# Mixture of experts inside a float32 network: tokens in groups of 32, expert weights unsplit and read once

## The chip, the cores and the metric

One core of one Trainium2 chip runs the whole program. The metric is device time in microseconds (us) of one execution, median of several; lower is better. Engines: PE is TensorE, DVE is VectorE, ACT is ScalarE, POOL is GpSimd, SP is SyncE, which only starts transfers here.

## The reference, cut to what matters

Two blocks run one after the other in float32 on 256 latent tokens of 1024 features (and 256 context tokens in part of the first block). The change is in one place only, the mixture of experts that ends the first block:

```python
def _moe_swiglu(h, router_w, router_b, w1, w3, w2):
    logits = (h @ router_w) + router_b
    top_vals, top_idx = lax.top_k(logits, 2)
    top_w = jax.nn.softmax(top_vals, axis=-1)
    gates = jnp.sum(one_hot(top_idx, 8) * top_w[..., None], axis=-2)
    out = jnp.zeros_like(h)
    for e in range(8):
        out = out + gates[..., e:e + 1] * ((silu(h @ w1[e]) * (h @ w3[e])) @ w2[e])
    return out
```

h is 256 x 1024; w1[e] and w3[e] are 1024 x 2816, w2[e] is 2816 x 1024. Each token uses two of eight experts, so there are 512 pairs of token and expert, spread over the experts as the data has it. The eight experts hold 276.8 MB of weights.

## The kernel before

All of the network before and after the experts is a stream of weight tiles of 128 x 1024 float32 (`w_raw`). For every tile ACT writes a rounded copy in the type fp32r (`w_hi`, line 265), DVE writes the remainder (`w_lo`, line 269), and PE multiplies three times (`pe_triple`, lines 306 to 308: hi by hi, lo by hi, hi by lo); the sum of the three fp32r products stands in for one product in float32.

**Routing.** `dve_router` finds each token's two experts and its slot. Slots lie in blocks of 128: eight blocks, one for each expert, and three overflow blocks that an expert with more than 128 pairs takes (NBLK = 11, 1408 slots). `onehot` holds the token-by-slot matrices. `pe_gather` multiplies tokens by `onehot` and so gathers every slot's token vector, once for the hi and once for the lo part (line 2192); ACT writes `x_hi` (line 2204), DVE `x_lo` (line 2214).

**Experts.** For each of the 11 blocks the weights of its expert are read from HBM again, in 66 tiles of 512 KB (`sp_experts`, line 2054, ring `mraw` of six tiles; the overflow blocks take their expert's number from the register `e0`). ACT and DVE split each tile into `mhi` and `mlo` (lines 2324 and 2328). On PE a block of 128 slots is stationary and the weights move, 512 columns at a time. A block has 11 steps of 256 hidden columns (`step`): `hidden` makes 8 x 3 matmuls, `turn` transposes the 256 gated columns of the step before in two transposes (line 2243), `out` makes 4 x 3 matmuls into the output. ACT and DVE make silu and product (lines 2337 and 2402) and the hi and lo parts of the turned values (lines 2341 and 2407). Loops: blocks outside, steps inside, and the order on every engine is written by hand in `step`; five steps of each block are written out, the rest is a hardware loop.

**Back to tokens.** The block's output, scaled by its gates (`gsl`, from `slot_gates`, line 2282), overwrites the block's part of `x_hi` and `x_lo`; `spread` multiplies it by the transposed one-hot matrix (`s_main`, `s_last`) and adds it up in PSUM (line 2262). `dve_experts_out` adds the sum into `hT`, and the norm behind it starts with ACT's `normx` and PE's line 530. The constants of the second block (`conb`) are loaded together with the slot numbers as the experts begin (`pool_conb`).

A place far from the experts matters as well: `pe_quad` (line 662), which makes the rows of the modulation at the start of the program. It puts 32 stationary columns each into four column groups of the array, one after another, and each group has plain float32 weights of its own moving through it.

Of the kernel before, what the change touches and what calls it, by code (L numbers as in the profile page):

```python
# [17 lines left out]
F32 = mybir.dt.float32  # L18
F32R = mybir.dt.float32r
# [23 lines left out]
NBLK = 11  # L43
SLOTS = NBLK * P
FSTEP = 256
NSTEP = DFF // FSTEP
XT = 6 * NSTEP
MOE_RAW = 6
MOE_RING = 4
# [29 lines left out]
for _n, _w in CONSTS_B:  # L79
# [6 lines left out]
          ("na_out", 8), ("moe", XT * NBLK)]  # L86
# [7 lines left out]
for _n, _w in STREAM:  # L94
# [3 lines left out]
MOE = XT * NBLK  # L98


SECOND = {"tok_ps": ("mod_ps", 1), "moe_rank": ("tot_ps", 1), "gat_hi": ("mb_ss", 1), "gat_lo": ("tm_ps", 1),
          "sp_ps": ("xtm_ps", 1), "x_acc": ("btm_ps", 1), "tok_hi": ("cv", 1), "x_hi": ("dt_l", 1),
          "y_hi": ("aneg", 1), "sp_sb": ("dt_u", 1), "moe_a": ("dt_rows", 1), "moe_mask": ("dt_abs", 1),
          "tok_lo": ("dt_w", 1), "x_lo": ("mb_sq", 2), "onehot": ("mb_ms", 1), "y_out": ("mb_done", 1),
          "slotno": ("lora", 32)}


def build(nc, io):
    with ExitStack() as es:
# [108 lines left out]
        def sp_stream(sp):  # L218
# [18 lines left out]
            repeat(sp, BASE["moe"], RING, more, first=first)  # L237
            sp_experts(sp)
            first = BASE["moe"] + MOE
            sp.wait_ge(tile_used.sem, first + RING)  # L240

            def later(n, j):
                slot = (first + j) % RING
                if not (isinstance(n, int) and n < first + RING):
                    sp.wait_ge(lo_ready.sem, n - (RING - 1))
                sp.dma_start(raw[:, slot, :], w[one(n - MOE)].rearrange("o p c -> p (o c)")
                             ).then_inc(raw_loaded[slot].sem, 16)
# [11 lines left out]
        rounds_apart = [0]  # L259

        def act_split(act, n, i3, slot):

            act.wait_ge(raw_loaded[slot].sem, i3 * 16 + (16 - rounds_apart[0] * 16))
# [1743 lines left out]
        def cb(name):  # L2007
            return conb[:, BCOL[name][0]:BCOL[name][1]]

        conb_at = END - 64 - (NCONB * 4 + 63) // 64 * 64  # L2010
        mhi = sb("mhi", [P, MOE_RING, 1024], F32R, at=ring0)
        mlo = sb("mlo", [P, MOE_RING, 1024], F32R, at=ring0 + 4096 * MOE_RING)
        slotno = sb("slotno", [P, SLOTS], at=ring0)
        tok_hi = sb("tok_hi", [P, 2, D], F32R, at=ring0 + 4096 * MOE_RING)
        tok_lo = sb("tok_lo", [P, 2, D], F32R, at=ring0 + 4096 * MOE_RING + 8192)
        s_at = ring0 + 8192 * MOE_RING
        s_last = sb("s_last", [P, 3, SEG], F32R, at=s_at)
        (lgt, t1, oh1, oh2, slt, msk, wv, ovf, oin, oex, dlt, eov, pq, xj, xi, gov, t24, gsl, _r) = lay(s_at + 3072, [
            ("lgt", [P, 2, NE]), ("t1", [P, 2, NE]), ("oh1", [P, 2, NE]), ("oh2", [P, 2, NE]), ("slt", [P, 2, NE]),
            ("msk", [P, 2, NE]), ("wv", [P, 8]), ("ovf", [P, NE]), ("oin", [P, NE]), ("oex", [P, NE]),  # L2020
            ("dlt", [P, NE]), ("eov", [P, NE]), ("pq", [P, 4]), ("xj", [P, 3]), ("xi_f", [P, 3]), ("gov", [P, 2, 3]),
            ("t24", [P, 3, NE]), ("gsl", [P, NBLK])])
        assert _r <= ring0 + 3 * 4096 * RING, _r
        x_at = area
        x_hi = sb("x_hi", [P, KT, SLOTS], F32R, at=x_at)
        x_lo = sb("x_lo", [P, KT, SLOTS], F32R, at=x_at + 4 * KT * SLOTS)
        mraw = sb("mraw", [P, MOE_RAW, 1024], at=x_at + 8 * KT * SLOTS)
        one_at = x_at + 8 * KT * SLOTS + 4096 * MOE_RAW
        onehot = sb("onehot", [P, 2, SLOTS], F32R, at=one_at)
        s_main = sb("s_main", [P, NE, SEG], F32R, at=one_at + 8 * SLOTS)  # L2030
        assert one_at + 8 * SLOTS + NE * SEG * 4 <= conb_at
        normx = sb("normx", [P, KT, SEG], at=x_at + 8 * KT * SLOTS)
        xi = sb("xi", [P, 3], mybir.dt.int32, at=s_at + 3072 + 6 * 64 + 6 * 32 + 2 * 32)
        xg_hi = sb("xg_hi", [P, 2, 2, P], F32R, at=g_at)
        xg_lo = sb("xg_lo", [P, 2, 2, P], F32R, at=g_at + 2048)
        xraw = deep_loaded
        GROUPS_X = ((0, 512), (512, 1024), (1024, SLOTS))
        PEEL = 5

        def spread_of(b):  # L2040
            return s_main[:, b, :] if b < NE else s_last[:, b - NE, :]

        def slots_of(b):
            return slice(b * P, (b + 1) * P)

        def sp_experts(sp):
            w = io["wexp"]

            def load(m, slot, idx):
                if not (isinstance(m, int) and m < MOE_RAW):
                    sp.wait_ge(lo_ready.sem, m + (BASE["moe"] - MOE_RAW + 1))
                sp.dma_start(mraw[:, slot, :], w[one(idx)].rearrange("o p c -> p (o c)")
                             ).then_inc(xraw[slot].sem, 16)
            sp.wait_ge(*S("arena_free2").next("sp"))
            before = None
            for b in range(NBLK):
                if b < NE:
                    e0 = b * XT  # L2060
                else:
                    if b == NE:
                        sp.wait_ge(*S("overflow").next("sp"))
                    e0 = sp.value_load(xi[0:1, b - NE:b - NE + 1], min_val=0, max_val=NE - 1) * XT
# [1153 lines left out]
```

## Time and profile before

| | |
|---|---|
| median of 3 runs | 3622.81 us (3614.82 to 3623.66) |
| profiled execution, span | 3619.5 us, 3.3 below the median |
| mean granted clock of TensorE | 0.967 |
| PE busy | 3402.0 us, 94% |
| DVE, ACT busy | 2497.9 us, 1878.7 us |
| HBM read | 719.57 MB, 199 GB/s over the span |
| expert weights read (`mraw`) | 726 transfers of 512 KB |

The profile has one execution. Its page gives no time of that execution beside the span, so sums are made against the span, and the 3.3 us between it and the median is carried along. PE's busy time overstates its use, because the ends of pipelined matmuls are modelled: the distance from one start to the next is the figure to read, and the timeline of PE has it. In a row of the timeline, two numbers lead: the start in the span and the time covered. One plain float32 matmul stands there as two records, one fp32r matmul or transpose as one.

### The profile page before, as it was taken

How to read it: one execution, taken by the hardware profiler on the slowest of the kernel's cores; microseconds unless marked ns; L12 is line 12 of the kernel's file. 1: busy time of each engine (PE TensorE's matmuls, PEld its weight loads, DVE VectorE, ACT ScalarE, POOL GpSimd, SP SyncE). 2: the span in 40 equal slices, each digit the busy share in tenths (PEclk: the TensorE clock that was granted, in tenths of full speed). 3: DMA queues.
4: the chain of work that ended last, by engine and by line, in shares of the span. 5: the costliest groups of instructions: out<-in, count | busy, mean ns of one | idle time of the engine just before them, and what ended most of it. 6: DMA issues, size and time to landing. Idle time of an engine off the chain costs nothing.

```text
span 3619.5 us, 70952 instructions
## 1 busy us (share of the span) xinstructions
PE 3402.0 (94%) x27148; PEld 3001.8 (83%) x27148; DVE 2497.9 (69%) x3327; ACT 1878.7 (52%) x2493; POOL 7.6 (0%) x17
## 2 busy tenths in 40 slices
PE   5987988899999988999999999999999999999998
PEld 3865857789898867888888888887998899998898
DVE  3778575555555367899999999997558555557555
ACT  3323231234444354788888888886445644444633
POOL 0000000000000000000000000000000000000000
PEclk8997989999999998999999999999999999999999
DMA  5225041035456303999999999996553354553354
GB/s 202 90 102 192 4 171 37 20 128 184 152 181 210 107 31 127 328 363 361 359 363 362 361 361 363 359 362 224 187 184 117 122 183 154 188 183 123 109 182 156
DMA packets 199351, 723.31 MB, mean 200 GB/s; under 512 B 21888, under 2 KB 25472, under 8 KB 198784
## 3 DMA queue, kind: packets, MB, share of 16 engines
q1 hardware_dynamic: 198576, 714.01, 55.4%
q0 software_dynamic: 592, 6.69, 0.5%
q8 instruction: 135, 2.21, 0.2%
q14 instruction: 48, 0.39, 0.0%
HBM read 719.57 MB, written 1.05 MB: 199 GB/s over the span
## 4 chain that ended last, share of the span: by engine, by line
PE 84%; DVE 9%; ACT 3%; DMA 2%; issue 1%; SPq 1%; DVEq 0%; ACTq 0%
PE ps L306 24%; PE ps L307 24%; PE ps L308 24%; DMA ada_late<-wada 1%; PE ps L1571 1%; PE ps L662 1%; PE ps L530 1%; PE ps L1568 1%; PE ps L1562 1%; PE ps L2243 1%; DVE w_lo L269 1%; PE ps L2192 1%; DVE tt L1659 1%; PE ps L2262 1%; ACT w_hi L265 1%
## 5 line engine op out<-in xcount | busy, mean ns | idle before, releaser
L269 DVE TENSOR_TENSOR w_lo<-w_raw,w_hi 128x1024 fp32r<-128x1024 f32 x529 | 647.4, 1225 | 717.8 <-ACT w_hi L265 714.4
L265 ACT ACTIVATE w_hi<-w_raw 128x1024 fp32r<-128x1024 f32 x529 | 558.6, 1059 | 794.2 <-PE ps L308 738.4
L306 PE MATMUL ps<-a_hi,w_hi 128*128 128x256 f32 (+1 forms) x3012 | 901.4, 299 | 54.1 <-DVE a_lo L557 24.6
L2328 DVE TENSOR_TENSOR mlo<-mraw,mhi 128x1024 fp32r<-128x1024 f32 x726 | 876.8, 1224 | 90.4 <-ACT mhi L2324 61.2
L308 PE MATMUL ps<-a_hi,w_lo 128*128 128x256 f32 (+1 forms) x3012 | 899.9, 299 | 0.0
L307 PE MATMUL ps<-a_lo,w_hi 128*128 128x256 f32 (+1 forms) x3012 | 899.8, 299 | 0.0
L2324 ACT ACTIVATE mhi<-mraw 128x1024 fp32r<-128x1024 f32 x726 | 770.6, 1062 | 178.9 <-PE ps L308 151.4
L306 PEld LDWEIGHTS ps<-a_hi,w_hi 128*128 128x128 f32 x3012 | 583.2, 194 | 78.0 <-issue 52.0
L307 PEld LDWEIGHTS ps<-a_lo,w_hi 128*128 128x128 f32 x3012 | 577.7, 192 | 16.5 <-issue 0.5
L308 PEld LDWEIGHTS ps<-a_hi,w_lo 128*128 128x128 f32 x3012 | 577.4, 192 | 14.7
L306 PE MATMUL ps<-mhi,x_hi 128*128 128x512 f32 x968 | 395.0, 408 | 1.9 <-DVE mlo L2328 1.9
L308 PE MATMUL ps<-mhi,x_lo 128*128 128x512 f32 x968 | 383.8, 397 | 0.0
L307 PE MATMUL ps<-mlo,x_hi 128*128 128x512 f32 x968 | 383.1, 396 | 0.0
L306 PE MATMUL ps<-g_hi,w_hi 128*128 128x256 f32 x1056 | 298.9, 283 | 4.5 <-DVE g_lo L465 4.5
L307 PE MATMUL ps<-g_lo,w_hi 128*128 128x256 f32 x1056 | 298.7, 283 | 0.0
L308 PE MATMUL ps<-g_hi,w_lo 128*128 128x256 f32 x1056 | 298.5, 283 | 0.0
L308 PEld LDWEIGHTS ps<-mhi,x_lo 128*128 128x128 f32 x968 | 182.6, 189 | 44.8
L306 PEld LDWEIGHTS ps<-mhi,x_hi 128*128 128x128 f32 x968 | 182.3, 188 | 39.3 <-issue 2.2
L307 PEld LDWEIGHTS ps<-mlo,x_hi 128*128 128x128 f32 x968 | 182.9, 189 | 37.8
L306 PEld LDWEIGHTS ps<-g_hi,w_hi 128*128 128x128 f32 x1056 | 202.2, 192 | 5.5 <-issue 5.5
L308 PEld LDWEIGHTS ps<-g_hi,w_lo 128*128 128x128 f32 x1056 | 202.3, 192 | 0.0
L307 PEld LDWEIGHTS ps<-g_lo,w_hi 128*128 128x128 f32 x1056 | 202.1, 191 | 0.0
(503 smaller groups left out, 4360.4 us busy)
## 6 DMA issues: line engine op xcount, KB each, us to landing
mraw<-wexp SPq DMA_DIRECT2D x726, 512.0 KB, 5.3
w_raw<-wstream SPq DMA_DIRECT2D x529, 512.0 KB, 3.3
ada_late<-wada SPq DMA_DIRECT2D x80, 512.0 KB, 6.1
ada_raw<-wada SPq DMA_DIRECT2D x16, 512.0 KB, 9.0
bia<-bias POOLq DMA_DIRECT2D x1, 4096.0 KB, 13.2
con<-consts SPq DMA_DIRECT2D x1, 1824.0 KB, 16.0
conb<-constsb POOLq DMA_DIRECT2D x1, 1224.0 KB, 8.0
hT<-ctxT SPq DMA_DIRECT2D x1, 1024.0 KB, 12.5
```

The costliest lines, as they stand in the source:

```text
L265: nc.scalar.activation(whi[:, slot, :], raw[:, slot, :], ACT.Copy).then_inc(hi_ready.sem, 1)
L269: nc.vector.tensor_tensor(wlo[:, slot, :], raw[:, slot, :], whi[:, slot, :].bitcast(F32), ALU.subtract).then_inc(lo_ready.sem, 1)
L306: nc.tensor.matmul(out, lhs[0], rhs[0], start=start, stop=False, skip_group_check=skip)
L307: nc.tensor.matmul(out, lhs[0], rhs[1], start=False, stop=False, skip_group_check=skip)
L308: return nc.tensor.matmul(out, lhs[1], rhs[0], start=False, stop=stop, skip_group_check=skip)
L530: last = nc.tensor.matmul(ps[:, 4, 0:SEG], ones[:], (work or normw)[:, k, :], start=(k == 0), stop=(k == KT - 1))
L662: last = nc.tensor.matmul(ps[32 * j:32 * j + 32, bank + half, :], cvp[:, k0 + j, :], tile[:, half * 512:(half + 1) * 512], start=(k0 == 0) ...
L1562: heads_of(d, lambda d, m, e: nc.tensor.matmul(ps[hp(e), d, col(m)], nl[hp(e), lv % 2, d, m, :], tt[hp(e), d, 0, m, :], start=True, stop=True)
L1568: heads_of(d, lambda d, m, e: nc.tensor.matmul(ps[hp(e), 2 + d, col(m)], tt[hp(e), d, 1, m, :], xs[hp(e), d, m, :], start=True, stop=True))
L1571: heads_of(d, lambda d, m, e: nc.tensor.matmul(ps[hp(e), 2 + d, col(m, 1)], xs[hp(e), d, m, :], tt[hp(e), d, 1, m, :], start=True, stop=Tr ...
L2324: nc.scalar.activation(mhi[:, slot, :], mraw[:, rslot, :], ACT.Copy).then_inc(hi_ready.sem, 1)
L2328: nc.vector.tensor_tensor(mlo[:, slot, :], mraw[:, rslot, :], mhi[:, slot, :].bitcast(F32), ALU.subtract).then_inc(lo_ready.sem, 1)
```

## The change

**Slots** lie in groups of 32 instead of blocks of 128: eight base groups, one for each expert, and NX = 15 extra groups, which go to whatever expert has more than 32, 64, ... pairs; 23 groups, 736 slots. Four groups side by side make a "quad" of 128 slots, so there are NQ = 6 quads, the last with three groups.

**Weights** are neither split nor read again. A "set" holds, for all eight experts at once, one piece of 128 x 512 float32 (2 MB, two transfers of 1 MB); there are 88 sets for the hidden layer (11 steps of 8) and 44 for the output (two halves of 22), 132 in all, in a ring of three. The matmuls are plain float32 with 32 stationary columns: in each set PE goes through the six quads (`quad`), and each group of a quad sits in its own column group, with its own expert's weights moving. The base groups read the set directly. Since the extra groups' experts are known only at run time, ACT and DVE copy their weights out of the set into `wx` first (6 copies of 128 x 512 on ACT, 9 on DVE for each set, in four parts), at an address held in a register. Quad i (i from 2) waits for part i-2; part j of the next set waits for quad j+2 of this one.

**Order.** The hidden layer of all slots comes first (`gT` keeps the turned values of all 736 slots and 2816 columns), then the output layer in two halves of 512 columns. At the end of each eight sets the six banks are emptied by silu and product, and in the first set of the next step `turn` puts two transposes behind each quad. `spread` of the first half runs between the sets of the second. `x`, hidden values and weights have no hi and lo parts any more; only the final `y_hi`, `y_lo` keep them. Nothing in the stage is a hardware loop. `conb` is loaded behind the experts.

```diff
-NBLK = 11
-SLOTS = NBLK * P
+GS = 32
+NX = 15
+SLOTS = (NE + NX) * GS
+NQ = 6
+SETS1 = NSTEP * KT
+SETS = SETS1 + 2 * FT
+SET_RING = 3
+X_ACT = ((0,), (4, 5), (8, 9), (12,))
+X_DVE = ((1, 2, 3), (6, 7), (10, 11), (13, 14))
...
+        def sp_set_free(sp, n):
+            sp.wait_ge(S("set_base").sem, based(n, 1))
+            sp.wait_ge(S("wx_act").sem, copied(X_ACT, n, 3))
+            sp.wait_ge(S("wx_dve").sem, copied(X_DVE, n, 3))
...
+            for n in range(SETS):
+                if n >= SET_RING:
+                    sp_set_free(sp, n - SET_RING)
+                for half in range(2):
+                    sp.dma_start(wsets[n % SET_RING][:, 4 * half:4 * half + 4, :].rearrange("p e c -> p (e c)"),
+                                 io["wexp"][2 * n + half]).then_inc(set_loaded[n % SET_RING].sem, 16)
...
+            def quad(n, i, lhs, first, last):
+                if i >= 2:
+                    pe.wait_ge(S("wx_act").sem, copied(X_ACT, n, i - 2))
+                    pe.wait_ge(S("wx_dve").sem, copied(X_DVE, n, i - 2))
+                for j in range(4 if i < NQ - 1 else 3):
+                    g = 4 * i + j
+                    w = wsets[n % SET_RING][:, g, :] if g < NE else wx[:, g - NE, :]
+                    done = nc.tensor.matmul(ps[32 * j:32 * j + 32, i, :], lhs[:, group(g)], w, start=first, stop=last,
+                                            skip_group_check=True)
+                done.then_inc(*S("set_base" if i < 2 else "set_more").one)
...
+            for s in range(NSTEP):
+                for k in range(KT):
+                    n = s * KT + k
+                    set_in(pe, n)
+                    for i in range(NQ):
+                        if s and k == 0:
+                            pe.wait_ge(*S("h_prod").next("pe"))
+                        quad(n, i, xT[:, k, :], k == 0, k == KT - 1)
+                        if s and k == 0:
+                            turn((s - 1) * NQ + i)
...
+            for h in range(2):
+                for f in range(FT):
+                    n = SETS1 + h * FT + f
+                    set_in(pe, n)
...
+                    for i in range(NQ):
...
+                        quad(n, i, gT[:, f, :], f == 0, f == FT - 1)
...
+                    if h == 1 and f < NQ:
+                        spread(f)
+            pe.wait_ge(*S("x_out").next("pe"))
+            for q in range(NQ):
+                spread(q)
...
+        def copies_of(n, j, evacuate, copy):
+            if n > 0 and j == 0:
+                for i in (0, 1):
+                    evacuate(n - 1, i)
+            if n > 0:
+                evacuate(n - 1, j + 2)
+            if n < SETS:
+                copy(n, j)
...
+            ids = {x: dve.value_load(xi[0:1, x:x + 1], min_val=0, max_val=NE - 1) for part in X_DVE for x in part}
+            def copy(n, j):
+                if j == 0:
+                    set_in(dve, n)
+                if n > 0:
+                    quad_done(dve, n - 1, j + 2)
+                for x in X_DVE[j]:
+                    nc.vector.tensor_copy(wx[:, x, :], wsets[n % SET_RING][:, one(ids[x]), :].rearrange("p o c -> p (o c)")
+                                          ).then_inc(*S("wx_dve").one)
```

`pe_gather` makes one sum of hi and lo in PSUM, for 512 and then 224 slots (32 matmuls each) instead of two sums for 512, 512 and 384 (96 matmuls).

On PE, in the middle of the expert stage of the kernel before, a turn and what follows it (`x_hi`, `x_lo`: slots; `mhi`, `mlo`: weights):

```order
L308 MATMUL ps<-mhi,x_lo 128x512
L2243 MATMUL ps<-ident,g_f 128x128 [waits g_f]
L2243 MATMUL ps<-ident,g_f 128x128
L306 MATMUL ps<-mhi,x_hi 128x512 [waits lo_ready]
L307 MATMUL ps<-mlo,x_hi 128x512
L308 MATMUL ps<-mhi,x_lo 128x512
```

The same place of the changed kernel, the end of the eighth set and the start of the ninth (`wset2`: the set itself, `wx`: copies, `mg`: gated hidden values, `y_pe`: the semaphore for the evacuated turn):

```order
L2239 MATMUL ps<-wx_167,xT_164 32x512 [waits wx_dve,wx_act]
L2239 MATMUL ps<-wx_167,xT_164 32x512 x2
L2239 MATMUL ps<-wset2_159,xT_164 32x512 [waits h_prod,deep_loaded2,mb_rt]
L2239 MATMUL ps<-wset2_159,xT_164 32x512 x3
L2250 MATMUL ps<-ident_61,mg_171 128x128 x2
L2239 MATMUL ps<-wset2_159,xT_164 32x512 [waits h_prod]
L2239 MATMUL ps<-wset2_159,xT_164 32x512 x3
L2250 MATMUL ps<-ident_61,mg_171 128x128 x2
L2239 MATMUL ps<-wx_167,xT_164 32x512 [waits wx_dve,wx_act,h_prod]
L2239 MATMUL ps<-wx_167,xT_164 32x512 x3
L2250 MATMUL ps<-ident_61,mg_171 128x128 [waits y_pe]
```

The three fp32r matmuls of 128 stationary columns are now four plain ones of 32, and a turn stands behind each quad of every eighth set.

On DVE, one set in the changed kernel (before, this engine's place held one `mlo` subtraction of 128x1024 for each tile, waiting for `hi_ready`):

```order
L2421 COPY wx<-wset_157 128x512 [waits set_more,deep_loaded0]
L2421 COPY wx<-wset_157 128x512 x2
L2421 COPY wx<-wset_157 128x512 [waits set_more]
L2421 COPY wx<-wset_157 128x512
L2421 COPY wx<-wset_157 128x512 [waits set_more]
L2421 COPY wx<-wset_157 128x512
L2421 COPY wx<-wset_157 128x512 [waits set_more]
L2421 COPY wx<-wset_157 128x512
```

Nine copies in four parts; each part waits for a quad of the set before (`set_more`), the first for the load as well (`deep_loaded0`).

## Rows read from the trace of the kernel before

**Rows 1.** The page: busy us of each engine, share of the span, instructions.

```profile
PE 3402.0 (94%) x27148; PEld 3001.8 (83%) x27148; DVE 2497.9 (69%) x3327; ACT 1878.7 (52%) x2493; POOL 7.6 (0%) x17
```

**Rows 2.** Windows: us, busy (count) of PE, PEld, DVE, ACT, POOL; PEclk, DMA share, GB/s.

```profile
1500.00:1700.00 200.00, 200.00 (x898) 162.24 (x897) 183.79 (x189) 160.66 (x189) 0.00 (x0) 1.00 0.98 362
```

**Rows 3.** Chain of waits inside the expert stage, shares by line.

```profile
by line: PE ps L306 31.5%; PE ps L308 31.4%; PE ps L307 31.2%; PE ps L2243 2.5%; PE ps L2262 1.4%; DVE mlo L2328 0.7%; DMA mraw<-wexp 0.7%; PE ps L2282 0.5%; PE ps L2272 0.1%; ACT mhi L2324 0.1%; DVE t L2173 0.1%; DVE gov L2174 0.1%; issue 
```

**Rows 4.** Timeline of PE around one turn: start us, us, engine, line, op, count [idle].

```profile
1701.93 0.40 PE L308 MATMUL ps<-mhi,x_lo 128*128 128x512 f32 x1
1702.17 0.38 PE L2243 MATMUL ps<-ident,g_f 128*128 128x128 f32 x2
1702.31 0.48 PE L306 MATMUL ps<-mhi,x_hi 128*128 128x512 f32 x1
1702.62 0.40 PE L307 MATMUL ps<-mlo,x_hi 128*128 128x512 f32 x1
```

**Rows 5.** Timeline of PE: gather, and start of the expert stage.

```profile
1408.74 1.19 PE L2192 MATMUL ps<-onehot,tok_hi 128*128 128x512 f32 x2 [5.85 <-DVE onehot L2154]
...
1412.15 0.62 PE L2192 MATMUL ps<-onehot,tok_hi 128*128 128x512 f32 x2
...
1425.21 0.51 PE L2192 MATMUL ps<-onehot,tok_hi 128*128 128x384 f32 x2
...
1432.89 0.47 PE L306 MATMUL ps<-mhi,x_hi 128*128 128x512 f32 x1 [1.87 <-DVE mlo L2328]
```

**Rows 6.** Timeline of PE at the end of the expert stage.

```profile
2496.45 0.39 PE L308 MATMUL ps<-mhi,xg_lo 128*128 128x512 f32 x1
2496.68 0.28 PE L2262 MATMUL ps<-s_main,x_hi 128*128 128x256 f32 x1
...
2503.32 3.62 PE L530 MATMUL ps<-normx,ones 128*128 128x256 f32 x16
```

**Rows 7.** Page, groups of the expert stage: busy us, mean ns | idle before, releaser.

```profile
L2328 DVE TENSOR_TENSOR mlo<-mraw,mhi 128x1024 fp32r<-128x1024 f32 x726 | 876.8, 1224 | 90.4 <-ACT mhi L2324 61.2
...
L2324 ACT ACTIVATE mhi<-mraw 128x1024 fp32r<-128x1024 f32 x726 | 770.6, 1062 | 178.9 <-PE ps L308 151.4
...
L306 PE MATMUL ps<-mhi,x_hi 128*128 128x512 f32 x968 | 395.0, 408 | 1.9 <-DVE mlo L2328 1.9
```

**Rows 8.** Timeline of PE and its weight loads at the early modulation rows (L662).

```profile
11.73 3.64 PE L662 MATMUL ps<-ada_raw,cvp 128*32 128x512 f32 x16 [11.73 <-DMA ada_raw<-wada]
16.81 1.92 PE L662 MATMUL ps<-ada_raw,cvp 128*32 128x512 f32 x16 [1.43 <-DMA ada_raw<-wada]
...
48.13 3.64 PE L662 MATMUL ps<-ada_raw,cvp 128*32 128x512 f32 x32
...
48.59 0.13 PEld L662 LDWEIGHTS ps<-ada_raw,cvp 128*32 128x32 f32 x4 [0.30 <-issue]
...
50.73 0.13 PEld L662 LDWEIGHTS ps<-ada_raw,cvp 128*32 128x32 f32 x4 [0.30 <-issue]
```

**Rows 9.** Timeline of PE where 64-column matmuls give way to 128-column ones.

```profile
252.89 0.38 PE L1192 MATMUL ps<-wm_b,xdt 128*64 128x128 f32 x2
253.11 0.38 PE L1194 MATMUL ps<-cm_b,hin 128*64 128x128 f32 x2
253.42 0.49 PE L1172 MATMUL ps<-bcx 128*128 128x128 f32 x2
```

**Rows 10.** Timeline of PE at the slot gates, and the clock of that stretch.

```profile
1468.25 3.63 PE L2282 MATMUL ps<-lgt,onehot 128*128 128x1 f32 x32
...
1460.00:1480.00 20.00, 20.00 (x106) 16.98 (x105) 12.06 (x13) 11.04 (x15) 0.00 (x0) 0.91 0.80 277
```

**Rows 11.** Lines with 128x512 float32 from SBUF to SBUF on DVE and ACT: ns min/median/max.

```profile
L1129 DVE TENSOR_SCALAR dd<-dd x8: 426/426/428, 239.4 to 284.3; 128x512 f32<-128x512 f32 x8
...
L574 ACT ACTIVATE normw<-hT x16: 613/616/635, 38.3 to 1166.5; 128x512 f32<-128x512 f32 x16
```

**Rows 12.** Windows: 10 us in which only loads ran (columns as in rows 2).

```profile
24.00:34.00 10.00, 0.00 (x0) 0.00 (x0) 0.00 (x0) 0.00 (x0) 0.00 (x0) 0.50 1.03 408
```

More of the change, by code:

```diff
@@ L2008, in cb @@
             return conb[:, BCOL[name][0]:BCOL[name][1]]
[L2010 to L2016, printed above, removed]
@@ L2048, in sp_experts @@
-        def sp_experts(sp):
[L2049 to L2055, printed above, removed]
-            sp.wait_ge(*S("arena_free2").next("sp"))
[L2057 to L2064, printed above, removed]
-                m = b * XT - 2 if b else 0
-                for q in range(4):
-                    load(m + q, (m + q) % MOE_RAW, e0 + q)
-                for q in range(2 if b else 0):
-                    load(m + 4 + q, (m + 4 + q) % MOE_RAW, before + (XT - 2 + q))
-                with sp.Fori(0, NSTEP - 1) as i:
-                    for j in range(6):
-                        load(i * 6 + (b * XT + 4 + j), (4 + j) % MOE_RAW, i * 6 + (e0 + (4 + j)))
-                before = e0
-            for q in range(2):
-                load(MOE - 2 + q, (4 + q) % MOE_RAW, before + (XT - 2 + q))
@@ L2186, in pe_gather @@
                     i = g * KT + k
[L2187 to L2190 removed]
+                    if i >= 8:
+                        pe.wait_ge(*S("x_act" if i % 2 == 0 else "x_dve").next("pe"))
+                    for tok in (tok_hi, tok_lo):
                         for tt_ in range(2):
[L2192 to L2194 removed]
@@ L2195, in pe_gather @@
-            pe.wait_ge(*S("x_hi").next("pe", 4))
-            pe.wait_ge(*S("x_lo").next("pe", 4))
+                            last = nc.tensor.matmul(ps[:, i % 8, 0:c1 - c0], tok[:, tt_, k * P:(k + 1) * P],
+                                                    onehot[:, tt_, c0:c1], start=(tok is tok_hi and tt_ == 0),
+                                                    stop=(tok is tok_lo and tt_ == 1))
+                    last.then_inc(*S("gat_ps").one)
+            pe.wait_ge(*S("x_act").next("pe", 4))
@@ new lines, in spread @@
+            def spread(q):
+                r = rows_of(q)
+                pe.wait_ge(*S("y_out").next("pe"))
+                for m in range(4):
+                    for part in (y_hi, y_lo):
+                        last = nc.tensor.matmul(ps[:, 6 + m // 2, m % 2 * SEG:(m % 2 + 1) * SEG],
+                                                part[r, q, m * P:(m + 1) * P], spr[r, q, :],
+                                                start=(q == 0 and m % 2 == 0 and part is y_hi),
+                                                stop=(q == NQ - 1 and part is y_lo), skip_group_check=True)
+                    if q == NQ - 1 and m % 2 == 1:
+                        last.then_inc(*S("x_acc").one)
```

552 lines of the change are left out of this document (252 added, 300 removed).

## The prediction, made before the changed kernel ran

> **What bounds the kernel now.** I read the page first, for which engine has most work: PE, 94% busy [rows 1]. Since that figure overstates a pipelined engine, I looked at windows inside the expert stage: PE is at 200.00 of 200 us with a granted clock of 1.00, while DVE is at 184, ACT at 161, and loads run at 362 GB/s, DMA share 0.98 [rows 2]. So four resources are near their ends, and the chain of waits has to say which one leads: 98% of its links are PE's own matmuls and turns, 0.7% loads, 0.7% DVE's `mlo` [rows 3]. The timeline gives PE's true pace: an fp32r matmul of 512 columns starts every 0.235 us [rows 4]. The stage has 121 steps x 36 = 4356 of them, 1024 us at that pace. With gather, turns and spreads it lasts from 1408.7 (first gather matmul, [rows 5]) to 2503.3 (end of the last spread, [rows 6]), 1094.6 us. ACT waited for PE (151 us) more than for loads, and PE waited for DVE for 1.9 us in all [rows 7]. The stage is PE's, with the split on ACT and DVE and the loads close behind.
>
> **The change, part by part.** The rest of the program is untouched, so I sum the stage anew from 1408.7, the same first matmul, because the routing chain before it keeps its number of operations.
>
> *The quads.* 132 sets x 6 quads = 792. The trace has this very instruction: `pe_quad` puts 32 stationary columns each into four column groups, plain float32, 512 columns moving. At 48.13 there are 32 records (16 matmuls) in 3.64 us; the groups of four weight loads start every (50.73 - 48.59) / 5 = 0.428 us [rows 8]. A matmul is two records, so four groups side by side take 2 x 0.428 = 0.856 us. Quads: 792 x 0.856 = 678.0 us. The sixth has three groups and takes the same. Per set that is 5.14 us on PE.
>
> *The turns.* 11 steps x 6 = 66. A turn's two transposes cost 0.14 us, and the matmul behind them 0.31 instead of 0.235, together 0.22 [rows 4]. New is the change between 32 and 128 stationary columns, twice a turn. The nearest row is a change from 64 to 128: two records take 0.31 where their equals take 0.22, so 0.09 [rows 9]. 0.22 + 0.18 = 0.40, x 66 = 26.4 us. Bounds: 0.22 (15 us) and, if each change lets the pipeline run empty as at the end of a burst (0.21, below), 0.64 (42 us). I take 0.40, the row of a change of width.
>
> *Gather.* 64 matmuls instead of 96. The first eight take 3.4 us as now, 24 follow at 0.233 us ((1425.21 - 1412.15) / 56), 32 have 224 columns, 0.11 each in proportion, and 1.0 us for the last evacuation [rows 5]: 3.4 + 5.6 + 3.5 + 1.0, so experts start at 1422.2 instead of 1432.9. No split is waited for at that point.
>
> *Smaller work on PE.* Spreads of the first half, 48 x 0.119 us (56 matmuls from 2496.68 to 2503.32, [rows 6]) = 5.7. One-hot transposes, 12 x 0.07 = 0.8. Slot gates, 46 plain matmuls = 92 records, between 0.03 us (a weight load of 32 columns in a group of four, [rows 8]) and 0.113 us (3.63 / 32, [rows 10]), so 3 to 10 us in all; I take 6, since they have one moving column and their own column groups. Ten changes of width, 1.8. The slot gates also cost clock: around them the mean granted clock is 0.91 over 20 us [rows 10], 1.8 us lost; I carry 2. Together 16.3 us.
>
> *Registers.* ACT and DVE read six and nine expert numbers into registers before their first copy. No row of either engine shows that. Lower bound 0, because quads 0 and 1 (1.7 us) need no copy; upper bound 12, nine loads at some 1.3 us, the price of a full 1024-column operation [rows 7]. I take 4.
>
> *Copies, off the path.* A SBUF-to-SBUF operation of 128x512 is 0.43 us on DVE and 0.62 on ACT [rows 11]: 9 x 0.43 = 3.8 and 6 x 0.62 = 3.7 us a set, inside PE's 5.14. Order matters more than load here: part 0 may start when quad 2 of the set before is done, 2.6 us before the new set, and is needed 1.7 us after its start, so each part has 3 us or so to spare. At the end of a step six silus, six products and six turned evacuations come in between. I followed ACT and DVE through it: the last copy of the step's first set is done about 3.5 us after that set's start on PE, and the last quad, held up by turns, needs it at 5.5. Cover holds; if it failed, each failure would be paid 11 times, not 132.
>
> *Loads.* Set n can be loaded once set n-3 is free, 2 us after its start, and has 13 us until it is needed. So only the rate counts. Nothing but loads running, the trace shows 408 GB/s [rows 12]; 2.097 MB then take 5.14 us, exactly the quads of one set. The turns give slack (8 sets take 43.5 us on PE, 386 GB/s), the last 44 sets give almost none. At 408, loads stay just behind PE, and I cost them at nothing.
>
> *Tail.* After the last quad: silence until ACT's and DVE's scaled evacuation of it, at most 0.7 us each by half of [rows 7], hand-offs 0.4, eight spread matmuls 1.0: 2.8. Before, the stretch from the last expert matmul was 6.9 us, counted in the 1094.6.
>
> Sum: 678.0 + 26.4 + 16.3 + 4 = 724.7; 1422.2 + 724.7 + 2.8 = 2149.7 instead of 2503.3. **That saves 353.6 us**: span 3265.9, and with the 3.3 us of the median, **3269 us**. The median's runs spread over 9 us; 0.3% (11 us) is what I count as no change.
>
> **Rivals.**
>
> *Loads lead.* Only 408 GB/s in a quiet stretch speaks for the cover; under PE, ACT and DVE the trace shows 362 at a DMA share of 0.98 [rows 2], though there PE set the pace. If 362 is the most that the loads give, 129 sets from 1431 on (when set 0 is free) take 270.5 MB / 362 = 747 us; plus 2 for landing, 5.1 for the last set and 2.8: 2188, or 3307 us. At 350: 3334. The Trainium skill, "HBM Reference" (Specifications), puts a core's share at about 358 GB/s, and well above that (about 425) for a core that streams alone; by its first figure the time would be this rival's, 3316. The trace's 408 sides with the second, in a stretch without compute. For it: demand is 386 to 408 and so close to the best seen. Chance 0.2.
>
> *Quads do not run into each other.* At [rows 8] quads follow without a wait between them. A burst of four passes took 1.92 us, not 4 x 0.428 = 1.71, so filling and draining cost 0.21. If the wait ahead of each quad of copies broke the stream, 792 x 0.21 = 166: 3435 us. Against: waits that are already met stand ahead of the matmuls of [rows 4] as well, and the pace stays. The Trainium skill, "TensorE: Matmul & The Clock Gate" (Part 3, Packing small matmuls), speaks against the change in this way: three column tiles gave 2.38 times one, not 3. By that figure, an estimate, a quad is 26% dearer, 855 us instead of 678, and the time 3446. In [rows 8] four groups start 0.428 us after the four before, over 16 matmuls, and 512 columns in two records of 0.428 leave no room for 26% more; I stay with the row. Chance 0.1.
>
> *DVE leads.* If copies from an address in a register run at the pace of the two-input subtraction (1.22 us for 1024 columns, 0.61 for 512, [rows 7]), DVE needs 5.5 us a set, 726 in all, plus about 45 for products, turned values and routing tables: with 4 for registers and 2.8 at the end the stage closes at 2200, or 3319 us. Chance 0.06.
>
> *The clock falls; slower than before.* The first burst of quads took 3.64 us for 16 records, twice the time of those at 48.13: half clock; the next one, 1.4 us later, ran at full clock [rows 8], so these matmuls brought it up. But the longest such run in the trace is 3.6 us, and single-column work let it fall [rows 10]. If the chip does not take plain quads for enough activity, each costs 1.71 us: 678 more, 3947 us. It decides above 353.6 / 678 = 52% of the stage at half clock; below that the change still gains. Chance 0.03.
>
> *The groups are not side by side*, so the change does not do what it says: 3036 matmuls x 0.856 = 2599 us, 5190 us in all. [rows 8] contradict it. Chance below 0.01.
>
> **How the numbers follow.** The forecast as worked out has 0.56, with a range of its own of 3250 (turns 0.22, registers 0) to 3290 (turns 0.64, registers 8); loads 0.2, to 3335; DVE 0.06, near 3319; quads apart 0.1, near 3435; clock 0.03; the rest, waits that I did not see, 0.05. A range from 3250 to 3345 holds the first three, 0.82. Faster takes everything but the clock and unseen mishaps: 0.96; same 0.01; slower 0.03.
>
> **What would show it.** Line 2239 should have 6072 records, starts of passes 0.43 us apart at clock 1.00, and no idle time on PE beyond some 10 us in the stage. Copies (L2421, L2361) should show 0.43 and 0.62 us, with DVE and ACT idle for PE. Loads should run at some 385 GB/s, with SP waiting for sets to come free; if PE waits for `wset<-wexp` instead, the loads lead. The gather should end near 1421. The forecast is wrong if passes are further apart, if PEclk is below 0.9 in the stage, or if DVE has no idle time.

## The result, and the profile after

Both kernels were measured on the same chip; the kernel before came out 4 us under the median given ahead of the prediction.

| | before | changed |
|---|---|---|
| median | 3618.82 us (3614.76 to 3623.66) | 3276.17 us (3265.9 to 3278.42, 4 runs) |
| ratio | | 0.9044, 95% interval 0.9026 to 0.9061 |
| profiled execution, span | 3619.5 us | 3274.9 us |
| HBM read | 719.57 MB | 615.50 MB |
| expert stage in the trace | 1408.74 to 2503.32, 1094.6 us | 1412.72 to 2162.96, 750.2 us |

The kernel is 343 us faster by the medians; 354 was forecast. The stage accounts for it: it is 344.3 us shorter, and the two profiled spans differ by 344.6. Outside it two differences cancel: this execution reached the stage 4.0 us later than the kernel before, and took 4.2 us less behind it. Both parts vary by more than that among the profiles below, whose code there is the same (1406.7 to 1418.1 us ahead of the stage, 1109.3 to 1116.8 behind it).

The page of the changed kernel, busy time of each engine (to [rows 1]):

```profile
PE 3057.1 (93%) x28680; PEld 2358.6 (72%) x28680; DVE 1984.7 (61%) x3616; ACT 1498.5 (46%) x2390; POOL 7.6 (0%) x17
```

Windows of the changed kernel, columns as in [rows 2]:

```profile
1405.00:1425.00 20.00, 14.59 (x67) 12.56 (x66) 12.51 (x35) 5.42 (x11) 0.00 (x0) 0.68 0.00 1
1425.00:1500.00 75.00, 69.69 (x670) 25.39 (x672) 45.73 (x135) 46.82 (x91) 0.00 (x0) 0.95 0.79 309
1500.00:1700.00 200.00, 200.00 (x1729) 61.13 (x1723) 131.78 (x370) 134.19 (x262) 0.00 (x0) 1.00 0.98 381
1700.00:1900.00 200.00, 200.00 (x1718) 60.91 (x1721) 131.02 (x368) 132.24 (x258) 0.00 (x0) 1.00 0.97 380
1900.00:2100.00 200.00, 200.00 (x1758) 65.34 (x1754) 126.35 (x350) 128.34 (x236) 0.00 (x0) 1.00 0.98 388
```

PE is as full as in [rows 2], at full clock, but DVE has fallen from 92% to 66% and ACT from 80% to 67%: the copies are a lighter load than the split was. The loads run at 380 to 388 GB/s with a DMA share of 0.97 or 0.98, and still PE has no idle time. By [rows 2] one might have read a DMA share of 0.98 at 362 GB/s as "full"; here the same share stands beside 388. So the share alone does not show how near the loads are to their limit.

The chain of waits from 1430 to 2150 (to [rows 3]), and the page's groups of the stage (to [rows 7]):

```profile
by line: PE ps L2239 95.0%; PE ps L2250 3.3%; PE ps L2281 1.0%; DVEq L2412 0.2%; PE ps L2260 0.2%; issue 0.1%; PE ps L2271 0.1%; DVE wx L2421 0.1%; DVEq L2421 0.0%
```

```profile
L2421 DVE COPY wx<-wset 128x512 f32 x1188 | 425.4, 422 | 223.2 <-PE ps L2239 212.5
L2361 ACT ACTIVATE wx<-wset 128x512 f32 x792 | 444.5, 621 | 215.1 <-PE ps L2239 210.6
L2239 PE MATMUL ps<-wx,xT 128*32 128x512 f32 x2640 | 378.6, 597 | 4.8 <-DVE wx L2421 4.8
...
L2239 PE MATMUL ps<-wset,xT 128*32 128x512 f32 x1408 | 231.2, 595 | 0.5 <-ACT xT L2220 0.5
```

Line 2239 has 2640 + 1320 + 1408 + 704 = 6072 records, as forecast. The chain holds no load at all. Both copying engines waited over 200 us for PE. PE waited 4.8 us for a copy, once, and 0.5 us for the gather's evacuation. Its quads have no other wait.

The timeline of PE shows that one wait, at the start of the stage (start us, us covered, then engine, line and operation, with idle time in brackets):

```profile
1412.72 1.19 PE L2209 MATMUL ps<-onehot,tok_hi 128*128 128x512 f32 x2 [5.41 <-DVE onehot L2171]
...
1417.90 0.62 PE L2209 MATMUL ps<-onehot,tok_hi 128*128 128x512 f32 x2
...
1426.76 1.92 PE L2239 MATMUL ps<-wset,xT 128*32 128x512 f32 x16 [0.53 <-ACT xT L2220]
1433.45 5.57 PE L2239 MATMUL ps<-wx,xT 128*32 128x512 f32 x27 [4.77 <-DVE wx L2421]
```

And DVE's, then ACT's, what they did while PE waited:

```profile
1426.27 0.39 DVE L2226 COPY xT<-ps 128x224 f32<-128x224 f32 x1 [0.50 <-PE ps L2209]
1432.21 3.11 DVE L2421 COPY wx<-wset 128x512 f32 x9 [5.55 <-issue]
```

```profile
1429.38 3.23 ACT L2361 ACTIVATE wx<-wset 128x512 f32 x6 [3.20 <-issue]
```

After two quads PE needs copies. DVE was silent for 5.55 us before its first one with nothing to wait for ("issue"); the only instructions there are its nine register loads, some 0.62 us each. ACT's six took 3.20 us, 0.53 each. While PE stood still its granted clock fell to the half level, and it stayed there for most of the four quads behind the wait (windows, columns as in [rows 2]):

```profile
1430.00:1435.00 5.00, 1.54 (x8) 0.46 (x12) 2.79 (x9) 2.60 (x6) 0.00 (x0) 0.64 0.01 3
1435.00:1440.00 5.00, 5.00 (x36) 1.51 (x31) 4.31 (x18) 3.04 (x6) 0.00 (x0) 0.67 0.69 256
```

From the first of these quads (1433.45) to the next set's first record, at 1438.44, PE took 4.99 us. The run with early register loads, below, has the same 27 records at full clock in 2.63 us. So the clock cost 2.4 us.

Timeline of PE where turns stand between quads:

```profile
1876.57 0.44 PE L2250 MATMUL ps<-ident,mg 128*128 128x128 f32 x2
1876.93 1.07 PE L2239 MATMUL ps<-wset,xT 128*32 128x512 f32 x8
1877.93 0.44 PE L2250 MATMUL ps<-ident,mg 128*128 128x128 f32 x2
1878.30 1.06 PE L2239 MATMUL ps<-wx,xT 128*32 128x512 f32 x8
```

One quad with its turn is 1878.30 - 1876.93 = 1.37 us. A set without turns takes 5.15 us (1467.40 to 1472.55), so a quad is 0.858 and a turn 0.51. The sixth turn of a step has 96 slots and is shorter: a whole step, from 1523.22 to 1567.39, takes 44.17 us, 2.97 more than eight sets, which is 0.495 a turn.

The end of the stage (to [rows 6]):

```profile
2157.12 0.39 PE L2281 MATMUL ps<-spr,y_hi 128*128 128x256 f32 x1
...
2162.84 0.28 PE L2281 MATMUL ps<-spr,y_lo 96*128 96x256 f32 x1
2162.96 3.62 PE L533 MATMUL ps<-normx,ones 128*128 128x256 f32 x16
```

Between the last quad and line 533, PE works through 48 spread matmuls without a gap, 5.84 us.

### The profile page after: what moved, and what is told of

The parts are those of the page before. It is cut to its first block, busy times and chain, and to the rows that moved or that the text cites. A ratio compares the mean times of both kernels' runs of the same rounds, so it can differ in the third digit from the quotient of the medians.

```text
span 3274.9 us, 70340 instructions
## 1 busy us (share of the span) xinstructions
PE 3057.1 (93%) x28680; PEld 2358.6 (72%) x28680; DVE 1984.7 (61%) x3616; ACT 1498.5 (46%) x2390; POOL 7.6 (0%) x17
## 3 DMA queue, kind: packets, MB, share of 16 engines
q0 software_dynamic: 528, 6.43, 0.5%
HBM read 615.50 MB, written 1.05 MB: 188 GB/s over the span
## 4 chain that ended last, share of the span: by engine, by line
PE 83%; DVE 10%; ACT 3%; DMA 2%; issue 1%; SPq 1%; DVEq 0%; ACTq 0%
PE ps L2239 21%; PE ps L309 16%; PE ps L310 16%; PE ps L311 16%; DMA ada_late<-wada 1%; PE ps L1574 1%; PE ps L533 1%; PE ps L665 1%; PE ps L1571 1%; PE ps L1565 1%; PE ps L2250 1%; DVE w_lo L272 1%; DVE tt L1662 1%; DVE rs L543 1%; ACT w_hi L268 1%
## 5 line engine op out<-in xcount | busy, mean ns | idle before, releaser
L2421 DVE COPY wx<-wset 128x512 f32 x1188 | 425.4, 422 | 223.2 <-PE ps L2239 212.5
L2361 ACT ACTIVATE wx<-wset 128x512 f32 x792 | 444.5, 621 | 215.1 <-PE ps L2239 210.6
L2239 PE MATMUL ps<-wx,xT 128*32 128x512 f32 x2640 | 378.6, 597 | 4.8 <-DVE wx L2421 4.8
L2239 PEld LDWEIGHTS ps<-wx,xT 128*32 128x32 f32 x2640 | 98.6, 110 | 196.3 <-issue 150.0
L2239 PE MATMUL ps<-wset,xT 128*32 128x512 f32 x1408 | 231.2, 595 | 0.5 <-ACT xT L2220 0.5
L2239 PE MATMUL ps<-wx,gT 128*32 128x512 f32 x1320 | 188.8, 592 | 0.0
L2239 PEld LDWEIGHTS ps<-wx,gT 128*32 128x32 f32 x1320 | 50.5, 110 | 102.3 <-issue 80.2
L2239 PEld LDWEIGHTS ps<-wset,xT 128*32 128x32 f32 x1408 | 54.5, 109 | 91.6 <-issue 89.8
```

Of the source, the lines that this page charges most:

```text
L2239: done = nc.tensor.matmul(ps[32 * j:32 * j + 32, i, :], lhs[:, group(g)], w, start=first, stop=last, skip_group_check=True)
L2361: nc.scalar.activation(wx[:, x, :], wsets[n % SET_RING][:, one(ids[x]), :].rearrange("p o c -> p (o c)"), ACT.Copy).then_inc(*S("wx_act").one)
L2421: nc.vector.tensor_copy(wx[:, x, :], wsets[n % SET_RING][:, one(ids[x]), :].rearrange("p o c -> p (o c)")).then_inc(*S("wx_dve").one)
```

## The experiments

All times of the stage below run from the first gather matmul to the first matmul of line 533, read from the trace. This is a sharper measure than the medians: two executions of the changed kernel gave 750.24 and 750.27 us, while its whole time varies by 12 us from run to run (3265.9 to 3278.4).

### What stands behind PE: narrower quads, and no copies

```diff
+                    cols = 512 if first or i < 4 else 64
-                    done = nc.tensor.matmul(ps[32 * j:32 * j + 32, i, :], lhs[:, group(g)], w, start=first, stop=last,
-                                            skip_group_check=True)
+                    done = nc.tensor.matmul(ps[32 * j:32 * j + 32, i, 0:cols], lhs[:, group(g)], w[:, 0:cols],
+                                            start=first, stop=last, skip_group_check=True)
```

> Quads 4 and 5 of every set move 64 columns in place of 512, except in the first contraction step of each accumulation; 7/8 of those two quads' products are left out. Every load, copy, turn and wait stays. TensorE's work in a set falls from 6 x 0.856 = 5.14 us to about 4 x 0.856 + 2 x 0.11 = 3.6 us, so over some 115 sets with narrow quads about 1.5 us each, 178 us, could go. Theory (the loads are hidden with room at 408 GB/s but not far above it): a set cannot come in under 2.097 MB / 408 GB/s = 5.14 us against a mean pace of 730.3/132 = 5.53 us now, so the time falls by about 50 us, to about 3224 us, and TensorE waits for the set's load. Rival 1 (380 GB/s, the mean rate of the changed kernel, is already the most the loads give): the time falls by 10 us at most. Rival 2 (the copies lead next: VectorE's nine copies took 3.11 us back to back, with its other work about 3.8 us a set): it falls by some 150 us or more, to about 3120 us, with the loads over 500 GB/s.

With three narrow quads (`i < 3`):

> As the run with two narrow quads, with three: quads 3, 4 and 5 move 64 columns except in the first contraction step of each accumulation; 7/8 of their products are left out. TensorE's work in a set falls to about 2.9 us. If a floor under the set's pace was reached in the run with two narrow quads (loads, or copies at 3.8 us), the time is the same here within 5 us and TensorE only waits longer. If TensorE was still the bound there, another 80 us or so goes.

Measured: 3217.27 us (ratio 0.8882, 0.8864 to 0.8901) with two narrow quads; one execution of 3216.05 us with three. The stage with two took 694.9 us (1414.08 to 2108.97), 55.4 less than the changed kernel's. Windows of the run with two narrow quads, then of the one with three:

```profile
1500.00:1700.00 200.00, 171.22 (x1870) 59.43 (x1866) 139.56 (x400) 141.84 (x283) 0.00 (x0) 1.00 1.00 412
1700.00:1900.00 200.00, 173.27 (x1874) 60.25 (x1870) 139.92 (x401) 142.50 (x283) 0.00 (x0) 0.99 1.01 416
1900.00:2100.00 200.00, 162.67 (x1876) 58.75 (x1872) 128.57 (x366) 131.87 (x244) 0.00 (x0) 0.99 1.01 416
```

```profile
1500.00:1700.00 200.00, 160.09 (x1888) 56.56 (x1880) 138.36 (x396) 139.63 (x280) 0.00 (x0) 0.96 1.01 414
```

Groups of PE in the run with two narrow quads (1430 to 2170):

```profile
L2240 PE MATMUL ps<-wset,xT 128*32 128x512 f32 x1395 | 173.1, 601 | 56.5 <-DMA wset<-wexp 54.7 <-DVE mg L2430 1.6
...
L2240 PE MATMUL ps<-wset,gT 128*32 128x512 f32 x704 | 85.9, 603 | 36.4 <-DMA wset<-wexp 36.4
```

The theory's fall came out, a little larger (about 50 us expected, 55.4 in the stage). PE now waits 91 us for loads, and taking a third quad's columns away changes nothing beyond noise: that stage took 693.6 us (1408.57 to 2102.22), 1.2 less, of which 0.9 is a shorter gather. So the floor is not PE's. Nor is it the copies': ACT and DVE are some 70% busy and wait for loads too. Nor is a late issue the cause: each transfer is issued 6.9 us before the one ahead of it has landed (median). It is the loads, at 412 to 416 GB/s. A set of 2.097 MB then needs 5.04 to 5.09 us. The changed kernel's sets without a turn take 5.15: the loads were hidden with 1 to 2% of room there, and with 0.45 us a set over the whole stage (730.36 / 132 = 5.53).

> The 15 copies of each set (nine on VectorE, six on ScalarE) and TensorE's waits for them are left out; the extra groups read the set's own slice instead, so those groups are multiplied by the wrong expert's weights. Theory (TensorE leads the set, the copies are hidden but for the start): only the start changes, where TensorE waited 4.77 us for the first copies and ran set 0 at half clock 1.6 us too long; the time falls by 5 to 6 us, to about 3270 us, and the pace of a set without turns stays at 5.15 us. Rival (the copies or their reading of the same SBUF columns slow TensorE or the loads): the pace falls too, each 0.1 us of it worth 13 us; if the copies led, to 3240 us or less.

```diff
-            sp.wait_ge(S("set_base").sem, based(n, 1))
-            sp.wait_ge(S("wx_act").sem, copied(X_ACT, n, 3))
-            sp.wait_ge(S("wx_dve").sem, copied(X_DVE, n, 3))
+            sp.wait_ge(S("set_more").sem, extended(n, 3))
...
-                    w = wsets[n % SET_RING][:, g, :] if g < NE else wx[:, g - NE, :]
+                    w = wsets[n % SET_RING][:, g % NE, :]
```

Measured: 3275.63 us (ratio 0.905, 0.9032 to 0.9069), no difference that can be told, where a fall of 5 to 6 us was expected. The stage took 749.2 us (1409.93 to 2159.11), 1.1 less. The start did change as expected (timeline of PE in this run):

```profile
1423.09 10.50 PE L2234 MATMUL ps<-wset,xT 128*32 128x512 f32 x92 [0.53 <-ACT xT L2218]
```

Two sets, 92 records, run through without a wait: 10.43 us to the first one-hot transpose, against 17.77 (1426.76 to 1444.53) in the changed kernel. But a wait of another kind came in (what PE's quads waited for, whole run; then what SP waited for):

```profile
  DMA wset<-wexp: 5.0, 8
```

```profile
SPq L2078 <- PE ps L2234: 640.3, 129, 41.4
```

Without copies a set is in use until its last quad, so its place in the ring comes free later. In the changed kernel SP waited for the last copy of a set (377.4 us for ACT's, 178.1 for DVE's), and that copy is made ahead of the quads. There a set's load is issued 13.07 us before PE starts on the set, and has landed 4.5 us before it (median; 2.25 at the least); without copies it is issued 10.1 us ahead and lands 0.85 us ahead (medians). So eight times a load came too late, 5.0 us, and each such wait also lets PE's pipeline run empty: the stretches that hold them are 7.1 us longer than in the changed kernel. That eats the 7.3 us gained at the start, and a gather 0.9 shorter is what is left. The copies, which one would count as pure extra work, free the ring early and cover the loads. DVE fell to 7% busy and ACT to 6%, and the pace did not move: where no load was late, the quads between the turns of one step and of the next take 37.04 us in both kernels (1475.21 to 1512.25 here, 1486.18 to 1523.22 there). So the copies did not slow PE.

### Are the four groups side by side?

```diff
-                for j in range(4 if i < NQ - 1 else 3):
+                for j in range((4 if i < NQ - 1 else 3) if first else 1):
```

> Each quad issues only its first group's matmul, except in the first contraction step of each accumulation; the other three groups' products (two in the last quad) are left out of the remaining steps. All loads, copies and turns stay. Theory (the four column groups run side by side and a quad costs what one group costs, 2 passes x 0.428 us = 0.856): the time stays within 5 us of the changed kernel's 3276 us. Rival (the four are only partly side by side, the 0.856 us holds some serial work of each): a quad gets shorter, by up to 3/4 if they were serial, until the loads' floor is reached, some 50 us faster or more.

Measured: 3277.37 us in one execution, stage 749.9 us (1413.43 to 2163.34), against 750.2. Window of this run:

```profile
1500.00:1700.00 200.00, 200.00 (x630) 51.60 (x628) 131.69 (x370) 134.20 (x261) 0.00 (x0) 1.00 0.97 381
```

630 matmul records where there were 1729, in the same 200 us. Three of four groups cost nothing at all: 0.3 us over 2023 matmuls left out. The Trainium skill, "TensorE: Matmul & The Clock Gate" (Part 3, Measured speedup vs the span model), has 2.38 for three column tiles of 512 columns. Nothing of that loss shows in this stream of quads, where four groups take the time of one.

### The turns and the register loads

The changed kernel ran again beside the three variants:

> The changed kernel itself, unedited, beside the three variants that follow, on the same chip. 3276 us as measured at first, within 0.2%.

Measured: 3276.46 us (ratio 0.9046, 0.9034 to 0.9058), stage 750.27.

> The 66 turns (two 128-column transposes after each of the first six quads of a step) are issued two at a time, after quads 1, 3 and 5 of the set, so that TensorE goes from 512-column passes to 128-column ones and back 33 times in place of 66. A quad with its turn took 1.37 us in the changed kernel, 0.51 over the quad's 0.856, while two transposes in a row in the kernel before had 0.22 us of pitch each pair. Theory (0.22 us of each turn is the transposes, the other 0.29 is the two changes of width): two turns in a row cost 0.44 + 0.29 = 0.73 in place of 1.02, so 33 x 0.29 = 10 us go, to about 3267 us. Rival (each transpose costs 0.25 us wherever it stands, as after a change of the stationary's width from 32 to 128 within the turn): nothing goes, and 3276 us stays. A third way: the first turn of a pair waits longer for nothing, but the copy that evacuates it comes later, and the next step's first quad waits; then it is slower by some us.

```diff
                         quad(n, i, xT[:, k, :], k == 0, k == KT - 1)
-                        if s and k == 0:
+                        if s and k == 0 and i % 2 == 1:
+                            turn((s - 1) * NQ + i - 1)
                             turn((s - 1) * NQ + i)
```

(and the same in the output layer's first set). Measured: 3263.99 us (ratio 0.9019, 0.9006 to 0.9031), stage 740.8 us (1416.28 to 2157.07), 9.5 less; 33 x 0.29 = 9.6 was expected. PE in this run:

```profile
1873.24 0.66 PE L2250 MATMUL ps<-ident,mg 128*128 128x128 f32 x4
1873.83 1.92 PE L2239 MATMUL ps<-wx,xT 128*32 128x512 f32 x16
1875.68 0.65 PE L2250 MATMUL ps<-ident,mg 128*128 128x128 f32 x4
1876.27 1.92 PE L2239 MATMUL ps<-wx,xT 128*32 128x512 f32 x14
```

Two quads and two turns are 1876.27 - 1873.83 = 2.44 us, 0.73 over the quads' 1.71, as expected. So a pair of changes of width costs 0.29 us, 0.15 each, where 0.09 was taken from [rows 9].

> The register loads of the extra groups' expert numbers (nine on VectorE, six on ScalarE) are made before these engines' evacuations of the gather, while TensorE's gather is not yet ready to be evacuated. Theory: TensorE's wait of 4.77 us for the first copies and the 1.6 us of half clock that followed it go, and the time falls by about 6 us, to about 3270 us. Rival 1: the register loads (about 5.5 us on VectorE, 3.2 on ScalarE) are only moved onto the path of the gather's evacuations, and the time stays. Rival 2: the waiting was for the copies' own work in set 0, not for the register loads, and at most 2 us go.

```diff
         def act_gather(act):
+            act.wait_ge(*S("extra_id").next("act"))
+            for x in (x for part in X_ACT for x in part):
+                ids_act[x] = act.value_load(xi[0:1, x:x + 1], min_val=0, max_val=NE - 1)
             for g, (c0, c1) in enumerate(GROUPS_X):
```

(likewise for DVE; the loads at the head of `act_experts` and `dve_experts` go). Measured: 3267.65 us (ratio 0.9027, 0.9015 to 0.904), stage 742.7 us (1406.74 to 2149.39), 7.6 less. Of this 0.9 lies in the gather, which took 13.16 to 13.18 us in this run, the one without copies and the one with three narrow quads, and 14.03 to 14.06 in the seven others. PE in this run:

```profile
1421.62 3.21 PE L2247 MATMUL ps<-wx,xT 128*32 128x512 f32 x27
1424.25 0.62 PE L2247 MATMUL ps<-wset,xT 128*32 128x512 f32 x1
...
1427.37 3.63 PE L2247 MATMUL ps<-wx,xT 128*32 128x512 f32 x30 [0.40 <-DVE wx L2426]
```

The first two sets take 11.03 us (1419.91 to 1430.94) in place of 17.77, 6.7 less: the wait of 4.77, the 2.4 of clock and some 0.2 of refilling are gone. Not all of the 7.3 comes back, since PE now waits 0.40 us for a copy of the second set. (The 1.6 us of the expectations set these records against four whole quads, 3.42 us; but the next set's first record starts before the last quad, which has three groups, is through.)

> Both edits together, turns in pairs and register loads early. If both theories hold the gains add, 10 + 6 = 16 us, to about 3260 us, provided that the loads keep up: a set at 5.14 us asks for 408 GB/s, and with two narrow quads the loads gave 412 to 416 GB/s, so the room is 1 to 2% in sets without a turn and the gain may be cut by a few us of waits for the load.

Measured: 3260.27 us (ratio 0.9008, 0.8995 to 0.902), stage 734.1 us (1414.16 to 2148.22), 16.2 less: 9.5 + 6.7. Its start, on PE, and DVE's copies:

```profile
1428.22 1.92 PE L2247 MATMUL ps<-wset,xT 128*32 128x512 f32 x16 [0.53 <-ACT xT L2225]
1429.94 3.21 PE L2247 MATMUL ps<-wx,xT 128*32 128x512 f32 x27
```

```profile
1422.26 2.60 DVE L2234 COPY xT<-ps 128x512 f32<-128x512 f32 x4 [5.85 <-PE ps L2209]
...
1428.04 3.10 DVE L2428 COPY wx<-wset 128x512 f32 x9
```

The register loads now lie in DVE's 5.85 us before its first evacuation (the row names PE, which had long been done), and the four evacuations follow at once. The gather took its usual 14.06 us: its first eight sums lie in PSUM banks of their own, so PE does not wait for late evacuations. PE waited for no load in this kernel, though from 1900 to 2025 they ran at 404 GB/s with a DMA share of 1.00. By the two ratios it takes 0.9958 of the changed kernel's time; their intervals (0.8995 to 0.902, 0.9034 to 0.9058) do not meet, so it beats both kernels.

> Register loads early, and the turns three at a time, after quads 2 and 5. By the width-change price that the pairs showed (0.22 us for a turn's transposes, 0.29 for the two changes of width: two quads with two turns took 2.44 us, 0.73 over the quads' 1.71), three turns in a row cost 0.66 + 0.29 = 0.95 us and 22 threes 20.9 us, against 24.1 for 33 pairs: 3 us less in the stage than with pairs, 731 us against 734.1. Against that: the turns go to two PSUM banks in alternation, so the third must wait until ScalarE has evacuated the first (0.38 us and the signals, from the end of the first, with 0.22 us of the second turn to hide it). Theory: that wait is 0.3 to 0.6 us, 22 times, 7 to 13 us, and the stage is 4 to 10 us longer than with pairs, 738 to 744 us. Rival: the wait is hidden, and the stage is 731 us.

```diff
-                        if s and k == 0 and i % 2 == 1:
-                            turn((s - 1) * NQ + i - 1)
-                            turn((s - 1) * NQ + i)
+                        if s and k == 0 and i % 3 == 2:
+                            turn((s - 1) * NQ + i - 2)
+                            turn((s - 1) * NQ + i - 1)
+                            turn((s - 1) * NQ + i)
```

(against the kernel with both edits; the same in the output layer's first set). Measured: one execution of 3271.26 us, stage 741.8 us (1417.49 to 2159.26), 7.7 longer than with pairs. PE in this run:

```profile
1874.90 0.66 PE L2258 MATMUL ps<-ident,mg 128*128 128x128 f32 x4
1875.81 0.44 PE L2258 MATMUL ps<-ident,mg 128*128 128x128 f32 x2 [0.26 <-ACT gT L2384]
1876.18 2.77 PE L2247 MATMUL ps<-wx,xT 128*32 128x512 f32 x22
1878.88 0.66 PE L2258 MATMUL ps<-ident,mg 128*128 128x128 f32 x4
1879.84 0.39 PE L2258 MATMUL ps<-ident,mg 96*128 96x96 f32 x2 [0.30 <-DVE gT L2444]
1880.15 1.92 PE L2247 MATMUL ps<-wset,xT 128*32 128x512 f32 x16
```

The third turn waits for the evacuation of the first, 0.26 to 0.30 us. Three quads and three turns take 1880.15 - 1876.18 = 3.97 us, 1.40 over the quads' 2.57 and 0.45 over the 0.95 without a wait: a wait that PE sees costs the refilling of its pipeline too. A whole step takes 44.01 us (1830.89 to 1874.90) against 43.31 with pairs (1821.08 to 1864.39), 0.70 more, and eleven steps make the 7.7 us. With two banks, two is better than one or three.

## Why the prediction was right, and where its terms were off

**The bound.** PE led, as the chain of [rows 3] and the sum had it. All three waits that might have taken its place (loads, DVE, ACT) stayed hidden, the loads with less room than the others. The quads take 680 us where the fp32r matmuls took 1024, and these 344 us are the stage's whole gain. They come from the count: 6 quads in place of 11 blocks for each of 132 pieces of weights. One piece for 128 slots costs more than before, 0.858 us against 3 x 0.235 = 0.705, but needs no split. No run takes the two halves of the change apart.

**The quads** were right to 0.3%. 0.856 us was read from 32 records of another use [rows 8], and 792 of them came at 0.858 (679.8 us in place of 678.0). That the four groups run side by side was shown by leaving three of them out.

**The turns** were the largest term that came out too low: 0.51 us in place of 0.40 (0.495 with the shorter sixth), 32.7 us instead of 26.4, inside the bounds of 0.22 and 0.64. The step that was mis-sized is "The nearest row is a change from 64 to 128 ... so 0.09": between four column groups of 32 and 128 columns, with plain passes of 512 columns on the one side, it is 0.15. The run with pairs shows it. The same error sits in the spreads and one-hot transposes between sets: a set with eight spreads takes 6.43 us (2047.73 to 2054.16), 1.28 over a plain one, so six cost 7.7 us, and the twelve transposes cost 1.7. That is 9.4 us where 5.7 + 0.8 + 1.8 = 8.3 was forecast.

**Gather.** 14.04 us in place of 13.5. "The first eight take 3.4 us as now" failed: the clock was at half for 5.2 us (1412.72 to 1417.90), as the mean of 0.68 over the first window shows. Three of the ten profiles of the changed kernel and its variants have the 3.4 us (1406.74 to 1410.14 in the run with early register loads, say), and a gather of 13.17 us. All three began the gather before 1410, like the kernel before; the seven others began after 1412. Why the clock comes up sooner in those stays open. I had the gather start at the same time as before; here it began 4.0 us later, but the ten began between 1406.7 and 1418.1, so this says nothing of the change.

**Smaller work.** The slot gates were priced at 6 us and 2 us of clock. They took 0.82 us (92 records, 1456.60 to 1457.42) and the clock did not fall. The upper price and the clock came from [rows 10], where these matmuls had 128 stationary columns each and one column moving; in column groups of 32 they are 9 ns a record, below my lower bound of 0.03 us. This error of -7.2 us was luck for the total: it hid the turns' +6.3 and more.

**Registers.** I took 4 us; it was 4.8 of waiting, 2.4 of clock and some 0.2 of refilling, 7.3 by the first two sets of this kernel and of the one without copies (17.77 - 10.43). The place was right. What I had not priced is that a wait of 5 us at the start costs clock behind it.

**Tail.** 2.8 us forecast, 5.84 measured. I counted "eight spread matmuls" behind the last quad, but the code in front of me issues all 48 of them there (`for q in range(NQ): spread(q)`). The 40 others are 4.8 us of work. The silence I had put before them did not come: PE goes from the last quad to the spreads of quads finished earlier.

**The balance.** The stage took 750.2 us, 9.2 more than the 741.0 forecast. Turns +6.3, registers and the clock behind them +3.3, tail +3.0, quads +1.8, spreads and transposes +1.1, gather +0.5, slot gates and their clock -7.2 make +8.8; the remaining 0.4 is not traced. The time of 3276 us lies 7 above the forecast of 3269. So the mechanism held, and the sum came nearer than its terms did.

**The rivals.** *Loads lead* fell, but by little: its 362 GB/s was the pace that PE had asked for, and the measured limit is 412 to 416. The Trainium skill, "HBM Reference" (Specifications), gives about 358 GB/s as a core's share and about 425 for a core that streams alone. The runs side with the second, now beside working engines too; by the first, an estimate, the time would have been 3316. What the loads would do with the neighbouring core at work is not shown here. *Quads do not run into each other*: a set without turns takes 5.15 us, 0.858 a quad, so waits that are already met do not break the stream. *DVE leads*: copies through a register took 422 ns, the same as the 426 of [rows 11], not 610. *The clock falls*: 1.00 in every window from 1500 to the end of the stage. *Not side by side*: refuted by the run with one group.

## What to carry to other kernels

When one engine leads and three stand close behind, cost each of them for a step of the work, and find the next floor with a run that only lightens the leader; here that floor was 1 to 2% away in sets without a turn. Group small passes of another shape on PE, up to the number of PSUM banks that are there to take them; here a third pass for two banks cost more than it saved. Register loads belong where their engine is waiting anyway.

## What the runs showed that I had not expected

- Leaving out 1980 copies of 128x512 changed the time by nothing, and made loads late: a copy ahead of its use frees the source's place in the ring earlier.
- A load of a number from SBUF into a register costs about 0.62 us on DVE (5.55 / 9) and 0.53 on ACT (3.20 / 6). The profile counts it as "issue", and where a wait follows it even puts the time down to another engine.
- The DMA share stands at 0.97 to 0.98 from 362 to 388 GB/s, at 1.00 with 404 and no wait of PE, and at 1.00 to 1.01 with 412 to 416, where PE waits for loads.
- Plain float32 matmuls with one moving column take 9 ns a record when they go round the column groups with 32 stationary columns, against 113 ns in [rows 10] with 128.
